# First attention's causal mask: from TensorE matmuls to tables masked by VectorE, with the tables' transfers issued by ScalarE

## What is computed

```python
logits = jnp.einsum('bqhd,bshd->bhqs', q_blk, kb).astype(jnp.float32) * scale
logits = logits + jnp.transpose(cq_blk, (0, 2, 1))[..., None] - c_k[:, :, None, :]
logits = jnp.where(causal[None, None], logits, NEG)
probs = jax.nn.softmax(logits, axis=-1).astype(vb.dtype)
```

## Time and profile before

| | |
|---|---|
| median of 3 runs | 1211.96 us |
| profiled execution | 1212.24 us, span 1210.4 us |
| TensorE busy | 1192.0 us, 98% |
| VectorE, ScalarE, GpSimd busy | 615.2, 551.2, 505.2 us |
| TensorE's granted clock | 0.999 of full speed |
| fox attention, first to last scores | 128 to 179 us |
| dsa attention, first to last scores | 234 to 280 us |

### The profile page before, as it was taken

How to read it: one execution, slowest core, us unless ns; L and a number is a source line. 1 busy time by engine, 2 the same in 40 slices (tenths; PEclk the granted TensorE clock), 3 DMA queues, 4 the chain that set the end, 5 groups by cost and what they waited for, 6 DMA issues and landing times.

```text
span 1210.4 us, 15678 instructions
## 1 busy us (share of the span) xinstructions
PE 1192.0 (98%) x5842; PEld 992.5 (82%) x5842; DVE 615.2 (51%) x1461; ACT 551.2 (46%) x991; POOL 505.2 (42%) x279
## 2 busy tenths in 40 slices
PE   9999999999999999999999999999999999999998
PEld 8878778888888887799878788888888888888886
DVE  5789864774628264994963673944222231220002
ACT  6453574476522364545775785434322332221113
POOL 1428462345433424125252883443344434443441
PEclk9999999999999999999999999999999999999999
DMA  8204662302332523143123204222332333323221
GB/s 275 81 25 142 172 175 70 105 1 71 122 105 70 186 93 105 35 161 106 36 40 83 92 9 163 95 95 94 105 104 71 105 105 99 100 80 122 97 77 70
DMA packets 80475, 119.19 MB, mean 98 GB/s; under 512 B 16008, under 2 KB 42760, under 8 KB 80016
## 3 DMA queue, kind: packets, MB, share of 16 engines
q1 hardware_dynamic: 80400, 118.19, 30.0%
HBM read 107.67 MB, written 4.21 MB: 92 GB/s over the span
## 4 chain that ended last, share of the span: by engine, by line
PE 85%; DVE 5%; POOL 3%; ACT 3%; issue 2%; DMA 1%; SPq 1%; ACTq 0%; DVEq 0%; POOLq 0%
PE bank L1724 64%; PE bank L2045 9%; PE bank L1820 2%; PE bank L1788 2%; PE bank L1802 2%; PE bank L1866 2%; DVE sc L1424 2%; DVE m L1420 1%; PE bank L1764 1%; POOL w_lo L704 1%; POOL w_lo L687 1%; PE bank L1905 1%; ACT w_hi L807 0%; DMA w_raw<-in_w_in 0%; POOL mK L741 0%
## 5 line engine op out<-in xcount | busy, mean ns | idle before, releaser
L687 POOL TENSOR_TENSOR w_lo<-w_raw,w_hi 128x2048 fp32r<-128x2048 f32 (+4 forms) x80 | 357.8, 4473 | 580.0 <-ACT w_hi L775 522.6
L1724 PE MATMUL bank<-aH,w_hi 128*128 128x512 f32 x800 | 318.3, 398 | 1.9 <-DVE mqT L1599 1.1
L1724 PE MATMUL bank<-aH,w_lo 128*128 128x512 f32 x800 | 311.9, 390 | 0.0
L1724 PE MATMUL bank<-aL,w_hi 128*128 128x512 f32 x800 | 308.7, 390 | 0.0
L775 ACT ACTIVATE w_hi<-w_raw 128x2048 fp32r<-128x2048 f32 (+4 forms) x76 | 140.7, 1851 | 263.0 <-PE bank L1724 162.2
L1724 PEld LDWEIGHTS bank<-aL,w_hi 128*128 128x128 f32 x800 | 150.2, 188 | 32.3
L1724 PEld LDWEIGHTS bank<-aH,w_hi 128*128 128x128 f32 x800 | 150.7, 188 | 31.0 <-issue 3.2
L1724 PEld LDWEIGHTS bank<-aH,w_lo 128*128 128x128 f32 x800 | 150.6, 188 | 26.5 <-issue 0.2
L1173 DVE TENSOR_TENSOR fg<-bank,rB 128x512 f32<-128x512 f32 x22 | 15.1, 691 | 128.2 <-PE bank L1724 128.2
L1724 PE MATMUL bank<-w_hi,aH 128*128 128x512 f32 (+4 forms) x224 | 77.1, 344 | 1.0 <-ACT aH L1034 0.7
L1724 PE MATMUL bank<-w_lo,aH 128*128 128x512 f32 (+4 forms) x224 | 75.4, 337 | 0.0
(11 more groups left out here) (338 smaller groups left out, 2119.9 us busy)
## 6 DMA issues: line engine op xcount, KB each, us to landing
w_raw<-in_w_in SPq DMA_DIRECT2D x23, 1024.0 KB, 5.1
w_raw<-in_w_gate SPq DMA_DIRECT2D x22, 512.0 KB, 3.8
w_raw<-in_w_up SPq DMA_DIRECT2D x22, 512.0 KB, 4.8
w_raw<-in_w_down SPq DMA_DIRECT2D x11, 1024.0 KB, 4.9
w_raw<-in_w_merge SPq DMA_DIRECT2D x8, 1024.0 KB, 4.9
w_raw<-in_w_out SPq DMA_DIRECT2D x8, 1024.0 KB, 5.0
w_raw<-in_w_ple_gate SPq DMA_DIRECT2D x4, 1024.0 KB, 4.9
w_raw<-in_w_in SPq DMA_DIRECT2D x4, 512.0 KB, 7.4
```

The costliest lines, as they stand in the source:

```text
L687: pool.tensor_tensor(out=w_lo[:, c % 2, 0:n], in0=w_raw[:, c % 2, 0:n], in1=w_hi[:, c % 2, 0:n].bitcast(F32), op=ALU.subtract).then_inc(w_ ...
L1724: ins = pe.matmul(o, l, r, start=(kk == 0 and operand == ROUNDED and m == 0), stop=(kk == total - 1 and operand == REST), skip_group_check ...
```

## The change

VectorE adds the mask to the bias tables instead of TensorE to the scores. A head's table becomes eight blocks of 128 keys: 0: c0; 1: c1 masked; 2 to 5: c0, c1, c2, c3 masked; 6: c2 masked; 7: c0 masked. A first transfer fills blocks 2 to 5, a second block 0; three additions (`MASKED_FROM`) make the masked blocks. For query blocks 0 to 3 the reduce reads block 7; blocks 0 and 1; blocks 0, 3 and 6; blocks 2 to 5 (`BIAS_OF`). The tables of even and odd heads are two tiles. `mask_bias(0)` stands ahead of the attention; `mask_bias(h + 1)` is issued when `fox_bias` is asked for head h's fourth unit, that is after VectorE's wait for that unit's scores and before its reduce. `load_cum` moves from SP to ScalarE: heads 0 and 1 between the second and third eviction of the vb projection, head h from 2 on at unit 4(h - 1), after L849 and before the exponential. The mask matmuls and the two bf16 tiles go.

```diff
+MASKED_FROM = ((1, 7, 5, 3, 5, 1), (5, 6, 1, 5, 6, 1), (7, 8, 1, 2, 3, 1))
+BIAS_OF = ((7, 8, 1), (0, 2, 1), (0, 7, 3), (2, 6, 1))
...
-        cB = place("cB", 98, [P, 2, S])
+        cB = [place(f"cB{i}", at, [P, 2 * NB, P]) for i, at in enumerate((98, 127))]
...
-            def load_cum(h):
-                sp_.dma_start(cB[:, h % 2, :], cum_dram[h:h + 1, :].broadcast_to([P, S])).then_inc(cum_landed[h % 2], 16)
-
...
                     sp_.wait_ge(cum_stored, 16)
-                    for h in range(2):
-                        load_cum(h)
...
                         wait_emptied(sp_, "fox.l", NB * (h - 1) - 1)
-                        load_cum(h)
                         stack_head(h)
...
+            def load_cum(h):
+                for first, n in ((2, NB), (0, 1)):
+                    row = cum_dram[h:h + 1, 0:n * P].broadcast_to([P, n * P])
+                    dst = cB[h % 2][:, first:first + n, :].rearrange("p c k -> p (c k)")
+                    act.dma_start(dst, row).then_inc(cum_landed[h % 2], 16)
+
...
+                    if name == "fox" and i % NB == 0 and NB <= i < NU - NB + 1 and i // NB + 1 < H:
+                        wait_emptied(act, "fox.l", i - 1)
+                        load_cum(i // NB + 1)
...
             for b in range(NB):
+                if b == 2:
+                    act.wait_ge(cum_stored, 16)
+                    for h in range(2):
+                        load_cum(h)
                 wait_filled(act, "vb", b)
...
-            dve.tensor_copy(ident16[:], ident[:])
-            dve.tensor_copy(diag16[:], tab("causal")[:, 3 * P:4 * P]).then_inc(half_ready, 1)
...
+            def mask_bias(h):
+
+                dve.wait_ge(cum_landed[h % 2], 32 * (h // 2 + 1))
+                for o0, o1, o_step, i0, i1, i_step in MASKED_FROM:
+                    t, given = cB[h % 2][:, o0:o1:o_step, :], cB[h % 2][:, i0:i1:i_step, :]
+                    n = i1 - i0
+                    mask = tab("causal")[:, 3 * P:4 * P].rearrange("p (o k) -> p o k", o=1).broadcast_to([P, n, P])
+                    dve.tensor_tensor(out=t, in0=given, in1=mask, op=ALU.add).then_inc(bias_masked, 1)
+
             def fox_bias(h, b):
                 if b == 0:
-                    dve.wait_ge(cum_landed[h % 2], 16 * (h // 2 + 1))
-                return cB[:, h % 2, 0:(b + 1) * P]
+                    dve.wait_ge(bias_masked, 3 * h + 3)
+                if b == 3 and h + 1 < H:
+                    mask_bias(h + 1)
+                first, end, step = BIAS_OF[b]
+                return cB[h % 2][:, first:end:step, :]
...
+            mask_bias(0)
             softmax("fox", sp, pT, fox_bias, low_rows, attB)
...
-                        if name == "fox":
-                            ins = pe.matmul(o[:, b * P:(b + 1) * P], ident16[:], diag16[:], start=False, stop=True,
-                                            skip_group_check=True)
                         fills(ins, name + ".l", i)
...
-            pe.wait_ge(half_ready, 1)
```

More of the change, by code:

```diff
@@ L21 @@
 F32R = mybir.dt.float32r
-BF16 = mybir.dt.bfloat16
 ALU = mybir.AluOpType
@@ L315, in build @@
         ident = sb("ident", [P, P])
-        ident16 = sb("ident16", [P, P], BF16)
-        diag16 = sb("diag16", [P, P], BF16)
+        sb("pad0", [P, P])
         ones = sb("ones", [P, P])
@@ L441, in build @@
         gains_landed, cst_landed, small_landed, p_landed = sem("gains_landed"), sem("cst_landed"), sem("small_landed"), sem("p_landed")
-        ones_ready, half_ready = sem("ones_ready"), sem("half_ready")
+        ones_ready, bias_masked = sem("ones_ready"), sem("bias_masked")
         sq_ready, sum_ready, rt_ready = sem("sq_ready"), sem("sum_ready"), sem("rt_ready")
@@ L1250, in softmax @@
                         wait_filled(dve, name + ".l", i)
+                        shaped = [t[:, 0:n] if name != "fox" else t[:, 0:n].rearrange("p (c k) -> p c k", k=P)
+                                  for t in (sc_[:, i % RING, :], bank_of(name + ".l", i))]
                         empties(dve.tensor_tensor_reduce(
-                            out=sc_[:, i % RING, 0:n], in0=bank_of(name + ".l", i)[:, 0:n], in1=k_bias(h, b),
+                            out=shaped[0], in0=shaped[1], in1=k_bias(h, b),
                             scale=1.0, scalar=-3e38, op0=ALU.add, op1=ALU.max, accum_out=mx[:, i:i + 1]),
```

## The result

The changed kernel takes 1222.56 us (median of 6 runs, 1220.57 to 1224.9) beside 1212.19 us (1211.73 to 1214.09) for the kernel before: ratio 1.0086, 95% interval 1.0076 to 1.0096, so 10.4 us slower (9.2 to 11.6). The profiled execution took 1221.47 us, span 1219.7.

What follows compares the result with a forecast made beforehand. TensorE bounds on average, but the loop VectorE, SP, copies, TensorE would bound the first attention: weight load +2.65 us, less 0.12 for unit 31, plus 0.3 for GpSimd, +2.8 us, so 1214.8 us (8 in 10: 1211.2 to 1218.0).

Steps and rivals of the forecast that it cites:

- the loop: First attention: VectorE's fourth reduce, SP's issues, copies, TensorE become the bound; two heads take 14.4 us against TensorE's 12.9.
- The matmuls' 3.8 us: First attention: 32 mask matmuls leave TensorE at 0.12 us a unit, 3.8 us gained if nothing else comes late.
- The wait on the table: Ahead of a head's fourth reduce, VectorE waits about 0.9 us for the next table in steady heads, before contention.
- T: The start of a head's first score matmul on TensorE, from which the forecast counts times within that head.
- Copies under contention: SP's copies of a head, meeting ScalarE's table transfers, take 6.23 us to the head's start instead of 5.93.
- a bound of 1.1 us: The table's 320 KB at 286 GB/s: the most that table transfers and copies can delay each other.
- I let it land with the first.: The table's second, smaller transfer, issued 0.42 us after the first, was taken to land with it at T + 6.3.
- The weight load: Load issued behind head 7's copies, at 169.97 us before: 2.65 us later, at about 172.6.
- VectorE's additions: 24 additions on VectorE, three a head, 0.77 us a head, ahead of the fourth reduce.
- a bound of 1.3: Additions meeting GpSimd's work in heads 5 and 6: up to 1.3 us more; 0.3 taken once.
- Rival C: SP's and ScalarE's issues take turns: 1217.3 us, chance 0.15; sign: issues beyond 0.6 (SP) or 0.34 us (ScalarE).
- Rivals A and B: A: the loop without contention, 1212.7 us, chance 0.27; B: the gain stays, 1208.2 us, chance 0.13 with its partial form.

Runs made afterwards that it cites:

- e6: Changed kernel with one table transfer a head from ScalarE, block 0 copied by VectorE, additions still ahead of the reduce: 1217.6 us, ratio 1.0049.
- e1: Kernel before with the 32 mask matmuls left out and nothing in their place: 1210.29 us beside 1212.57, ratio 0.9985.
- e10: Kernel before plus an unused 64 KB transfer a head in six heads, 32 rows of 2 KB, issued by SP before the copies: 1213.29 us, ratio 1.001.
- e2: Kernel before with its one table transfer a head issued by ScalarE instead of SP, mask still by TensorE: ratio 1.0005.
- e14: Changed kernel with one table transfer a head from ScalarE, block 0 copied by VectorE, additions behind the fourth reduce: 1213.24 us, ratio 1.0012.
- e3: Changed kernel with both table transfers a head issued by SP ahead of the copies, additions unmoved: 1220.75 us, ratio 1.0069.
- e4: Changed kernel with mask_bias(h + 1) put behind head h's fourth reduce and negated maximum, ScalarE still issuing both transfers: ratio 1.0045.

## Why the prediction was wrong

I forecast 1214.8 us (range 1211.2 to 1218.0); it is 1222.56. The direction and the loop were right, and its terms too small. The step that failed is the price of the meeting transfers. Of the 7.8 us between forecast and result, 4.5 go when the second transfer goes (e6); the other 3.3 stay with one transfer a head, 1.15 of them in the weight load's landing (6.40 us in e6, 5.25 before).

- *TensorE is the bound on average, the reduce of a head's fourth unit in this stage.* Right; the chain of the changed kernel runs through units 7, 15 and 23.
- *The matmuls' 3.8 us are eaten by the loop.* Right; the step was right too (6.43 us a head in e1), and even with no other edit they give 1.8 us.
- *The wait on the table.* Nearly right. Forecast T + 6.7 for its landing and T + 8.15 for the reduce's end. Measured for head 3: 155.08 - 148.24 = T + 6.8, and T + 8.4. I had the first issue too late (T + 2.8; it was at T + 2.0) and its landing too short (3.9 us from first issue; 4.8), and the two errors cancelled. For unit 7 only the second was there: the reduce ended at 140.10, not 138.75.
- *Copies under contention, 6.23 us from first issue to the head's start.* The step that failed. It was 148.24 - 140.13 = 8.1 us for head 3 and 164.31 - 156.67 = 7.6 us for head 5: +1.9 and +1.4. In head 5, 0.6 of this is one stretched issue of SP (0.93 us at 157.81, and 0.43 us idle behind it); the rest, and all of head 3's, is landing: 4.99 and 3.94 us for the last copy, where it was 2.81. I priced the meeting by bytes against DMA engines that were busy 0.9 of the time and took 0.3 of a bound of 1.1 us. The bytes do not explain it: the second transfer, 64 KB in 128 short rows, costs 4 to 4.5 us of time in this kernel, and in e10 the same bytes in long rows put nothing on the copies' landing. No run gave the changed kernel this transfer in long rows, so how much of the 4.5 us is the rows' and how much an extra transfer's is not shown.
- *"I let it land with the first."* The sentence in which the second transfer's price vanished. It was the longer of the two, 4.5 against 3.8 us.
- *The weight load.* I shifted its issue by 2.65 us and left its landing at 5.25. Its issue came 7 us later, 4.3 us more than forecast (1.35 from unit 7's reduce, 1.9 from head 3's copies, 1.7 from the loop to head 5, 0.6 from unit 23's reduce, less 1.2 in SP's issues behind it, most of it the issue of 1.41 us, which took 0.46 now), and its landing took 7.43 us: +2.2 that I had not asked about, with ScalarE's last tables in flight beside it.
- *VectorE's additions.* 0.83 us where I said 0.77. The meeting with GpSimd took 0.7 us (170.97, 1.53 us) where I took 0.3 of a bound of 1.3. The Trainium skill (SBUF — State Buffer, "SBUF: two separate sides") has it that VectorE with two SBUF inputs and GpSimd hold a shared pair of ports in turn, for whole instructions; the 1.51 us beside GpSimd's pair work agree.
- *Rival C, issuing engines exclude each other.* Not borne out. SP's issues beside ScalarE's took 0.60 us but for the one of 0.93, and the kernel before, where nobody else issues, has such ones too (0.78 us at 146.88, 1.41 at 165.26). In e2, e6 and e14 each of ScalarE's 18 table issues from 130 us on overlaps one of SP's, and all took 0.33 to 0.35 us. Only ScalarE's second, small one reached 0.70 us, beyond the 0.34 that I had named as C's sign; issued by SP (e3) it takes 0.43. The rule of a generator locked for one issuer at a time, of the Trainium skill (Perfetto Trace Analysis, "DMA Instruction — HWDGE (DVE, Sync)"), is not borne out by these rows; ScalarE's longer second issues leave room for it.
- *Rivals A and B.* Neither: the waits stand in most heads.
- *Where the clock would be* I did not ask. It fell, and in the changed kernel it did not matter.

What stays open: why the weight load takes 2 us more, and why 128 rows of 512 bytes leave the DMA engines without work; the runs show that they do, and not what makes them. Nor was the collision of ScalarE's queue with SP's, 1 to 2 us, taken apart further, nor the clock's part in e4.

## What to carry to other kernels

Where a loop through a transfer closes once a head, each of its terms is paid once a turn, so a small extra transfer on that loop must be priced by its landing and by what it does to those behind it, and not by its bytes. Ask of every added instruction whether it stands ahead of the one that releases a queue: here the same additions cost 4 us ahead of it and could hide, in part, behind it. And before giving a removed matmul its length, run the removal alone.

## What the runs showed of the hardware

- A transfer of 64 KB in 128 rows of 512 bytes took 4.0 us to land and put 0.7 us on the copies behind it (3.4 against 2.7 us); in 32 rows of 2 KB it took 3.5 us and put nothing on them. With the short rows the DMA engines were busy 0.2 to 0.4 for some 1.75 us.
- One table transfer a head issued by ScalarE, beside SP's issues, took 0.33 to 0.35 us to issue in all 18 cases, and SP had one to three stretched issues in those runs (0.74 to 1.77 us), and two in the kernel before (0.78 and 1.41 us). The last copies of each head landed later (fK from kbT 3.3 to 3.7 us against 2.7 to 2.8), the first ones sooner (fQ from qbT 2.3 to 2.5 us against 3.1), with no table ahead of them in SP's queue.
- Behind TensorE's wait of 2.97 us the granted clock was 0.65 and 0.50 in the next two stretches of 2 us; behind waits of 0.91 to 1.53 us in the same run it stayed at 1.00. The wait's length alone does not decide: it fell behind one of 1.96 us (e6) and stayed at 1.00 behind one of 2.74 us (e4).
- A VectorE addition of 256 columns with both inputs in SBUF took 1.51 us instead of 0.42 while GpSimd subtracted 512 columns beside it.
